# Attention slots with minima, biases added on GpSimd, and a division folded into the transposing matmul; decay and recurrent gates moved ahead of the index slots

## What is computed

```python
h = rms_norm(x, mix_norm)
x_r, g_r, q_b, c_kv, q_i, k_i, w_i, q_c, k_c, v_c, f_c, gate_a, gate_b, gate_c = split(h @ w_in)
o_a = rglru(x_r, g_r)        # conv of width 4, two gate matmuls, a scan over time
o_b = dsa(q_b, c_kv, ...)    # index scores relu(q_i.k_i) weighted by w_i, top 64 of them,
                             # softmax(ql.c * s + t5 bias, unselected at -1e30) @ c
o_c = fox(q_c, k_c, v_c)     # softmax(q.k * s + cum[t] - cum[key], causal) @ v
merged = sigmoid(gate_a)*(o_a @ w_b[0]) + sigmoid(gate_b)*(o_b @ w_b[1]) + sigmoid(gate_c)*(o_c @ w_b[2])
x = x + merged @ w_out
```

## Time and profile before

| | |
|---|---|
| median of 3 runs | 1520.07 us (1519.02 to 1524.56) |
| the profiled execution's own time | 1522.54 us |
| its span, first to last instruction | 1520.7 us |
| PE busy | 1448.3 us (95%) |
| DVE busy | 940.7 us (62%) |
| ACT busy | 785.6 us (52%) |
| POOL busy | 52.6 us (3%) |
| granted PE clock, mean over the span | 0.984 of full speed |

### The profile page before, as it was taken

How to read it: one execution, slowest core, us unless ns; L and a number is a source line. 1 busy time by engine, 2 the same in 40 slices (tenths; PEclk the granted TensorE clock), 3 DMA queues, 4 the chain that set the end, 5 groups by cost and what they waited for, 6 DMA issues and landing times.

```text
span 1520.7 us, 26191 instructions
## 1 busy us (share of the span) xinstructions
PE 1448.3 (95%) x9061; PEld 1290.7 (85%) x9061; DVE 940.7 (62%) x1501; ACT 785.6 (52%) x1396; POOL 52.6 (3%) x124
## 2 busy tenths in 40 slices
PE   6999999899999999999999999998999999999997
PEld 5888889788889897888878888888898898888886
DVE  5665655678665555666566666467875565565664
ACT  5555555644544455445465555456455445554553
POOL 1010000000000100000000000000000001000000
PEclk9999999899999999999999999999999999999999
DMA  7687655334424535566556666543353345356661
GB/s 224 192 201 218 201 150 157 117 116 141 138 91 162 192 112 163 173 189 193 167 175 186 193 185 199 158 141 112 112 166 111 111 170 164 112 172 192 190 193 70
DMA packets 286088, 243.60 MB, mean 160 GB/s; under 512 B 14281, under 2 KB 263545, under 8 KB 285985
## 3 DMA queue, kind: packets, MB, share of 16 engines
q1 hardware_dynamic: 283856, 236.77, 51.4%
q10 hardware_dynamic: 1600, 4.25, 0.8%
q0 software_dynamic: 528, 1.26, 0.6%
HBM read 241.18 MB, written 1.27 MB: 159 GB/s over the span
## 4 chain that ended last, share of the span: by engine, by line
issue 90%; PE 5%; POOLq 2%; POOL 1%; DMA 1%; DVE 0%; ACTq 0%; ACT 0%; DVEq 0%
PE work L1492 2%; PE work L1494 1%; PE acc L1454 1%; POOLq L685 1%; POOL diag L686 1%; POOLq L680 1%; DMA fb<-in_forget_bias 0%; POOLq L682 0%; DMA rows_dram<-brow_dram 0%; PE acc L1392 0%; DMA brow_dram<-brow 0%; POOL t L699 0%; POOL rstd L683 0%; DVE brow L1131 0%; ACTq L829 0%
## 5 line engine op out<-in xcount | busy, mean ns | idle before, releaser
L489 DVE TENSOR_TENSOR w_lo<-raw,w_hi 128x1024 fp32r<-128x1024 f32 x444 | 532.3, 1220 | 167.7 <-ACT w_hi L481 166.8
L1492 PE MATMUL work<-act,w_hi 128*128 128x512 f32 x1408 | 497.0, 397 | 2.6 <-DVE act L1031 2.6
L481 ACT ACTIVATE w_hi<-raw 128x1024 fp32r<-128x1024 f32 x444 | 453.4, 1053 | 39.0 <-PE acc L1454 26.4
L1494 PE MATMUL work<-act,w_lo 128*128 128x256 f32 x1408 | 395.0, 281 | 0.0
L1417 PE MATMUL work<-act,w_hi 128*128 128x256 f32 x1696 | 319.5, 287 | 9.0 <-DVE o_lo L1291 5.3
L1492 PEld LDWEIGHTS work<-act,w_hi 128*128 128x128 f32 x1408 | 264.2, 188 | 66.8 <-DVE act L1031 1.8
L1417 PEld LDWEIGHTS work<-act,w_hi 128*128 128x128 f32 x1696 | 270.3, 194 | 15.8 <-issue 9.6
L1494 PEld LDWEIGHTS work<-act,w_lo 128*128 128x128 f32 x1408 | 266.0, 189 | 1.5
L1417 PE MATMUL work<-act,w_lo 128*128 128x256 f32 x848 | 241.4, 285 | 0.0
L1417 PEld LDWEIGHTS work<-act,w_lo 128*128 128x128 f32 x848 | 164.3, 194 | 0.1
L741 ACT ACTIVATE gu_s<-work 128x256 f32<-128x256 f32 x176 | 58.0, 382 | 201.7 <-PE work L1494 201.7
(11 more groups left out here) (222 smaller groups left out, 1725.2 us busy)
## 6 DMA issues: line engine op xcount, KB each, us to landing
raw<-in_ffn_w_gu SPq DMA_DIRECT2D x176, 512.0 KB, 5.0
raw<-in_w_in SPq DMA_DIRECT2D x52, 1024.0 KB, 5.2
raw<-in_ffn_w_down SPq DMA_DIRECT2D x44, 1024.0 KB, 5.0
raw<-in_w_branch SPq DMA_DIRECT2D x12, 1024.0 KB, 5.0
raw<-in_w_mkv SPq DMA_DIRECT2D x8, 1024.0 KB, 5.0
raw<-in_w_out SPq DMA_DIRECT2D x8, 1024.0 KB, 5.0
raw<-in_w_mq SPq DMA_DIRECT2D x4, 1024.0 KB, 5.1
raw<-in_w_mo SPq DMA_DIRECT2D x4, 1024.0 KB, 4.8
```

What stands on the lines that cost most here:

```text
L481: eng.activation(halves(w_hi, slot, kind, part), halves(raw, slot, kind, part), ACT.Copy)\
L489: eng.tensor_tensor(halves(w_lo, slot, kind, part), halves(raw, slot, kind, part), halves(w_hi, slot, kind, part).bitcast(F32), ALU.subtra ...
L1492: pe.matmul(work[:, 2 * c + g, :], w_hi[:, slot, at_w:at_w + P], act[:, :, k, :], start=(k == 0), stop=False, skip_group_check=True)
L1494: mm = pe.matmul(work[:, 2 * c + g, 0:SEQ], w_lo[:, slot, at_w:at_w + P], act_hi[:, k, :], start=False, stop=(k == KT - 1), skip_group_che ...
```

## The change

- **Attention, DVE.** All logits are kept with the opposite sign, so that the row minimum is the bias of the exponential (`scale=-1.0`): `nm` comes straight from one `tensor_reduce` with `min`, and the negation goes. In fox the query's own `cum` is left out, since it is the same for all keys of a row and falls out of the softmax; `cum`, the job `cumT` and its copy go. POOL adds the causal mask to the second half of `fox_bias` once for each of the four pairs of heads, so slots with 256 keys need no mask on DVE; those with 128 keys add it in one instruction for both heads. In dsa POOL adds `t5` and `score` one slot ahead into `t5_score`.
- **Attention, division.** DVE only takes the reciprocal. POOL forms `over_sum`, a diagonal matrix of 1 / sum for each head (128 x 2 x 128), and PE multiplies the exponentials by it in ordinary matmuls in place of the transposes by the identity. PE's wait for `p_ready` becomes one for `over_sum_ready`.
- **Index stage.** `chan` moves behind `xr0`, and the convolution is done in two halves behind `xr0` and `xr1`. `rg` 0 and 1 and `fT` move ahead of `qi0`, `rg` 2 and 3 and `cT` ahead of `qi1`. The decay (sigmoid, running sum, store and broadcast load) and the gates' arithmetic on ACT and DVE move with them. The eight index slots now have a unit behind each second one. `dots` waits only for the half of `qi` that it reads, `qk` likewise. `rg_i` and `rg_a` lie over `merged` instead of `mem_x`.
- **Order of units.** `qc0, kc0, qc1, kc1` in place of `qc0, qc1, kc0, kc1`; `qb0, qb1` ahead of `ga0, ga1, ba0`. SP issues the loads in the new order; their number and sizes stay.

```diff
-FILL = dict(enumerate(("vc0", "vc1", "ga0", "ga1", "ba0", "qb0", "qb1", "ga2", "ga3", "ba1", "gc0", "gc1", "bc0",
+FILL = dict(enumerate(("vc0", "vc1", "qb0", "qb1", "ga0", "ga1", "ba0", "ga2", "ga3", "ba1", "gc0", "gc1", "bc0",
...
-IDX_FILL = {0: "qc0", 4: "qc1", 5: "kc0", 6: "kc1"}
+IDX_FILL = {1: "qc0", 3: "kc0", 5: "qc1", 7: "kc1"}
...
+            def causal_bias(pr):
+                h = HEAD_PAIRS[pr][0]
+                heads = fox_bias[:, h:h + 3:2, P:SEQ]
+                g.tensor_tensor(heads, heads, causal[:, P:SEQ].unsqueeze(1).to_broadcast([P, 2, P]), ALU.subtract)\
+                 .then_inc(causal_ready, 1)
+            def bias_and_score(l, s):
...
+                g.wait_ge(lg_ready, l * STREAM + s - 1)
+                g.tensor_tensor(t5_score[:, s % 2, :, 0:s_len], t5[:, h:h + 3:2, SEQ - s_len:SEQ],
+                                score[:, blk, 0:s_len].unsqueeze(1).to_broadcast([P, 2, s_len]), ALU.add)\
+                 .then_inc(t5_score_ready, 1)
...
+                for s in range(STREAM):
+                    if s == 0:
+                        g.wait_ge(bias_landed, l * 32 + 32)
+                        causal_bias(0)
+                    g.wait_ge(ri_ready, l * STREAM + s + 1)
+                    g.tensor_tensor(over_sum[:, s % 2, :, :], ident[:].unsqueeze(1).to_broadcast([P, 2, P]),
+                                    ri[:, s % 2, :].unsqueeze(2).to_broadcast([P, 2, P]), ALU.mult)\
+                     .then_inc(over_sum_ready, 1)
+                    if 0 < s < 4:
+                        causal_bias(s)
+                    if 8 <= s + 1 < STREAM:
+                        bias_and_score(l, s + 1)
...
-                            e = a.activation(lg[:, s % 2, j, 0:s_len], lg[:, s % 2, j, 0:s_len], ACT.Exp,
+                            e = a.activation(lg[:, s % 2, j, 0:s_len], lg[:, s % 2, j, 0:s_len], ACT.Exp, scale=-1.0,
...
-                        v.reduce_max(mx[:, s % 2, :], lgs, AX_X)
-                        v.drain()
-                        v.tensor_scalar(nm[:, s % 2, :], mx[:, s % 2, :], -1.0, None, ALU.mult).then_inc(lg_ready, 1)
+                        v.tensor_reduce(nm[:, s % 2, :], lgs, AX_X, ALU.min).then_inc(lg_ready, 1)
...
-                        v.reciprocal(ri[:, s % 2, :], sm[:, s % 2, :])
-                        v.drain()
-                        v.tensor_tensor(lgs, lgs, ri[:, s % 2, :].unsqueeze(2).to_broadcast([P, 2, s_len]), ALU.mult)\
-                         .then_inc(p_ready, 1)
+                        v.reciprocal(ri[:, s % 2, :], sm[:, s % 2, :]).then_inc(ri_ready, 1)
...
-                        pe.wait_ge(p_ready, l * STREAM + k + 1)
+                        pe.wait_ge(over_sum_ready, l * STREAM + k + 1)
...
-                                mm = pe.transpose(ps(("pt", k))[:, col:col + P], lg[:, k % 2, j, c * P:c * P + P], ident[:])
+                                mm = pe.matmul(ps(("pt", k))[:, col:col + P], lg[:, k % 2, j, c * P:c * P + P],
+                                               over_sum[:, k % 2, j, :], start=True, stop=True)
```

More of the change, by code:

```diff
@@ L156, in mix @@
         self.norm(1)
-        for name in ("xr0", "xr1", "gr0", "gr1"):
+        self.w_unit("xr0")
+        self.job("chan")
+        for name in ("xr1", "gr0", "gr1"):
             self.w_unit(name)
@@ L162, in mix @@
         self.job_of["misc"] = "nat"
-        self.job("chan")
-        for name in ("qi0", "qi1"):
-            self.w_unit(name)
+        self.job(("rg", 0))
+        self.job(("rg", 1))
+        self.job("fT")
+        self.w_unit("qi0")
+        self.job(("rg", 2))
+        self.job(("rg", 3))
+        self.job("cT")
+        self.w_unit("qi1")
         for i in range(IDX_SLOTS):
             self.job(("dots", i))
[L168 to L175, removed]
             if i in IDX_FILL:
@@ L275, in block_kernel @@
         merged = at("merged", [P, KT, SEQ])
+        rg_i = at("rg_i", [P, BT, SEQ], over="merged")
+        rg_a = at("rg_a", [P, BT, SEQ], over="merged", skip=4096)
         final_gain = at("final_gain", [P, D], over="merged")
@@ L289, in block_kernel @@
         qi = at("qi", [P, BT, SEQ])
+        over_sum = at("over_sum", [P, 2, 2, P], over="qi")
+        t5_score = at("t5_score", [P, 2, 2, SEQ], over="qc")
         vc = at("vc", [P, TT, BW])
@@ L336, in block_kernel @@
         wi = at("wi", [P, TT, HEADS])
-        cum = at("cum", [P, TT, HEADS])
         top8 = at("top8", [P, 8])
@@ L628, in _ @@
                   .then_inc(misc_landed, 16)
-                for name in ("qi0", "qi1") + tuple(IDX_FILL.values()):
+                for name in ("qi0", "qi1") + tuple(IDX_FILL[i] for i in sorted(IDX_FILL)):
                     w_in(l, name, COL[name[:2]] + 256 * int(name[2]))
@@ L1181, in _ @@
-                v.drain().then_inc(xc_ready, 1)
-                for j in range(2):
-                    splits(v, split_lo, l, f"qi{j}")
+                conv(0)
+                splits(v, split_lo, l, "xr1")
+                conv(1)
+                v.drain().then_inc(xc_ready, 1)
+                splits(v, split_lo, l, "gr0")
+                splits(v, split_lo, l, "gr1")
+                wait_done(v, l, "nat")
+                v.tensor_copy(nat[:], ps("nat")[:, 0:TT * NAT].rearrange("p (a n) -> p a n", a=TT))\
+                 .then_inc(bank_of("nat"), 1)
@@ new lines, in _ @@
+                for tt in range(TT):
+                    v.wait_ge(rstd_ready, l * 12 + 5 + tt)
+                    v.scalar_tensor_tensor(out=c_nat[:, tt, :], in0=nat[:, tt, HEADS:HEADS + LAT], scalar=rstd[:, tt:tt + 1],
+                                           in1=kvg[:], op0=ALU.mult,
+                                           op1=ALU.mult).then_inc(c_ready, 1)
+                v.wait_ge(fl_ready, l + 1)
+                v.scalar_tensor_tensor(out=f_l[:], in0=f_z[:], scalar=0.0, in1=f_l[:], op0=ALU.min, op1=ALU.subtract)
@@ L1184, in _ @@
+                v.tensor_tensor(xr[:, :, 0:SEQ], rg_a[:], rg_a[:], ALU.mult)
+                v.drain()
+                v.scalar_tensor_tensor(out=xr[:, :, 0:SEQ], in0=xr[:, :, 0:SEQ], scalar=1.0, in1=rg_r[:],
+                                       op0=ALU.add, op1=ALU.mult).then_inc(rg_v, 1)
+                splits(v, split_lo, l, "qi1")
                 for i in range(IDX_SLOTS):
@@ L1572, in _ @@
                     s_len = P * (blk + 1)
-                    wait_jobs(pe, l, ["ki", "qi0", "qi1"], ("dots", i))
+                    wait_jobs(pe, l, ["ki", f"qi{m // 2}"], ("dots", i))
                     for j in range(2):
```

279 lines of the change are left out of this document (131 added, 148 removed).

## The result

The changed kernel takes 1483.81 us (median of 4 runs, 1479.98 to 1487.17), the kernel before 1519.82 us on the same chip (4 runs, 1519.02 to 1524.56). The ratio is 0.9756 [0.9724, 0.9788]: 2.4% faster, 36 us.

What follows compares the result with a forecast made beforehand. PE, busy 95% of the span, was taken as the bound, losing time to waits and its lower clock. Terms -15.5 - 1 + 13.4 - 11.4 - 10 = -24.5 us, from the median 1520.07 to 1496 us; range 1486 to 1508.

Steps and rivals of the forecast that it cites:

- The waits: PE's waits in both layers: -15.5 us in the index stage and -11.4 us in the stream.
- the first `pt`: Start of the stream: PE still waits there for the softmax chain through DVE and POOL, 1.4 us in each layer.
- the `o_lo` waits: Stream, PE's four waits on DVE's reading of `uv`: 5.3 us before, to shrink to 1.1 us together.
- `qi1` and `qc0`: Index stage, two narrow places for ACT; rival: ACT falls behind there, +8 us, 1504 us, chance 0.08.
- The clock: PE in index stage and stream: 13 us lost at the lower clock, most returning once waits go, -10 us.
- the rival in which it doesn't: Rival: PE's granted clock falls as before, the 10 us are missing, 1506 us; chance 0.18.
- `cumT`: Index stage: four small matmuls per layer go from PE, -1 us.
- hidden in 30 of 32 slots: Stream: POOL's `over_sum`, 1.1 us (0.5 to 2.0), costs PE nothing except in the first step of each layer.
- the blocking rival: Stream: DVE and POOL block one another, delaying `over_sum` or DVE's reads; +6 to +9 us, 1502 to 1505, chance 0.12.
- the spare of 2.7 us: Stream, step 4: time between DVE's reciprocal and PE's `pt`, said to suffice for `over_sum` at 1.1 or 2.0 us.
- Transposes become matmuls: Stream, PE: 96 transposes become 192 matmul instructions, 23.8 - 10.4 = +13.4 us; ends +10.4 and +23.
- the low end of the range: Transposes at +10.4 us, all clock back, first waits half as long: 1488.6 us, put at 1486 for roundings.

Runs made afterwards that it cites:

- dve_divide: Changed kernel with the softmax division back on DVE, PE transposing by the identity, no `over_sum`, POOL's next bias beside the product: 1482.03 us, 0.9738 of the kernel before.
- dve_divide_2: As `dve_divide`, but POOL starts the next slot's bias only when DVE's product is done: 1478.65 us, 0.9711 of the kernel before.
- dots_apart: Changed kernel with index units behind slots 0, 2, 4, 6 and head pairs reordered so neighbouring `dots` read the same half of the partitions: 1495.14 us, 0.9817.
- early_softmax: As `dve_divide`, with DVE doing slot 0's logits and minimum ahead of the split for the last index unit: 1479.06 us, 0.9711 of the kernel before.
- divide_ordered: As `dve_divide_2`, with DVE's first softmax early and half of some fillers' splits moved behind what PE waits for: 1481.07 us, 0.9715.

## Why the prediction was right in direction and too small

**Right, and of the right size.** The waits: -27.6 us for a predicted -26.9. So good a match is partly luck. After the change 5.7 us are left where 3.9 were forecast, since the first `pt` waits 1.8 us in place of 1.4, the `o_lo` waits are 1.6 in sum in place of 1.1, and 0.5 for `vc` had no term; the other way went small gaps that the earlier trace rows doesn't list, 33.3 us before in place of the 30.8 counted. The index stage runs without a gap, so ACT did make `qi1` and `qc0` in time. The clock: `rg` and the units together take 10.1 us less, for a predicted 10. Not all of that need be the clock, but the clock's own record agrees: the stretches at the lower clock in the mixing parts sum to 37.5 us before and 10.2 after, and the matmuls in them to 32.8 and 10.4 us; at the prediction's 0.41 lost per us that is 13.4 us before and 4.3 after, 9 us back. `rg` had run mostly at the lower clock (9.3 of its 11.5 us), in between waits; what is left lies behind the wait at the first `pt`. That most of the clock comes back once the waits are gone, the forecast's least certain term, held, and the rival in which it doesn't is out. The four runs of the changed kernel still differ by their mean clock: 0.991, 0.994, 0.996 and 0.997 go with 1487.17, 1484.91, 1482.70 and 1479.98 us, 1.2 us per 0.001. `cumT`: -1.1 for -1.

**Right for the wrong part.** `over_sum` is hidden in 30 of 32 slots, as said. But its price isn't one number. One ahead of a half of `split_lo` (two SBUF inputs), and one with such a half beside it:

```profile
334.76 0.61 POOL L737 TENSOR_TENSOR over_sum<-ident,ri 128x256 f32<-128x256 f32 x1 [6.60 <-DVE ri L1325]
```

```profile
326.28 1.88 POOL L737 TENSOR_TENSOR over_sum<-ident,ri 128x256 f32<-128x256 f32 x1 [5.89 <-DVE ri L1325]
...
326.48 1.21 DVE L493 TENSOR_TENSOR w_lo<-raw,w_hi 128x1024 fp32r<-128x1024 f32 x1
```

Undisturbed it takes 0.61 us, not the 1.1 worked out from the earlier trace rows; behind DVE it takes up to 1.88, and the median of the 32 is 1.51. The estimate by the Trainium skill (GPSIMD Engine Reference, Elementwise), 0.6 us, was the better one for the undisturbed product; the trace agrees with it in 12 of the 32 slots. The lock is there in both directions: POOL's 0.61 grows to as much as 1.88 us beside the split's 1.21, and DVE's product goes from 0.69 to 1.83 us beside POOL's 1.29. The Trainium skill (SBUF — State Buffer, two separate sides) says that such operations of the two engines exclude one another for a whole instruction, and that the one that starts first goes first; the traces agree on the first point. On the second the recorded starts need care: a split that starts 0.15 us ahead of POOL's record makes POOL's product 1.51 to 1.55 us long, one that starts 0.20 us behind it 1.88, and only one that starts 0.41 us or more behind leaves POOL its 0.61, with the split then at 1.21 to 1.28.

So the mechanism of the blocking rival is real and its price wasn't: the spare of 2.7 us from the earlier trace rows takes 1.88, and in the changed kernel POOL bears the delay nearly alone, for none of the 444 halves of `split_lo` takes more than 1.285 us (1.227 before). Nor is the blocking part of the wait at the first `pt`, where `over_sum` takes 0.61 us in both layers (start 296.16, `pt` at 296.90 in the first). Only with the product back on DVE did the blocking cost time, 3.2 us of waits (`dve_divide` against `dve_divide_2`).

**The terms that failed.** The mechanism held; what failed is the sum, in a term that it didn't have and in one that was too large. The excess is 35.4 - 24.5 = 10.9 us.

- **`dots`, -4.5 us, no term at all.** The prediction said that a unit stands behind each pair of `dots` and asked only what that does to ACT. It took the 64 matmuls as the same work at the same price. The trace of before had the warning, which I didn't read: twelve instructions of three slots in a row take 263.88 - 262.79 = 1.09 us, where the four of a slot alone take 0.64 (256.85 - 256.22).

```profile
256.22 0.71 PE L1575 MATMUL work<-ki,qi 64*128 64x128 f32 x4 [0.69 <-ACT qi L734]
256.85 0.38 PE L1417 MATMUL work<-act,w_hi 128*128 128x256 f32 x1
...
262.79 1.16 PE L1575 MATMUL work<-ki,qi 64*128 64x128 f32 x12
263.88 0.44 PE L1582 MATMUL work<-ident,c_nat 128*128 128x128 f32 x2
```

This is the largest part of the miss, and `dots_apart` shows how it hangs on the neighbours: with the two slots of a pair on the same half the 64 instructions take 12.2 us.
- **Transposes become matmuls, +13.4, measured +11.0.** The 192 instructions cost 23.4 us, for 23.8 predicted; the mistake is in what they replace. I took 0.108 us for each of the 96 transposes, from one slot with 256 keys in the middle of a burst; over all slots they took 12.4 us, 0.129 each. The row was the cheapest of its kind: the sixteen slots with four transposes took 0.43 to 0.53 us, 0.121 for each transpose on average, and those with two 0.146 for each, among them two right behind PE's wait (310.19 to 310.56 in the trace of before, 0.185 each).
- **Small jobs around them, -2.2 us**, in `cT`, `fT`, `pv`, `uv` and `ql`, no term. All of them ran at the full clock before too, so the clock isn't the cause. `cT` and `fT` make 0.9 of it: the two matmuls of `cT` counted 0.44 us ahead of a wait before and 255.26 - 255.12 = 0.14 us in a row with the next unit after. The other 1.3 us stay open; no run separates them.
- **Waits -0.7 and outside the mixing part -1.0 us**, neither larger than what single executions differ by.

Together 4.5 + 2.4 + 2.2 + 0.7 + 1.0 = 10.8 of the 10.9 us; the clock and `cumT` make the rest. All terms that failed lay on one side, and the low end of the range (transposes at 10.4, all clock, half the first waits) had no room for work that becomes cheaper without being touched.

**What the parts are worth.** The order of the index stage gives 1.7% of the 2.4% by itself. The folded division, which the prediction counted as the price of the change, isn't bought back by what DVE saves: with the product back on DVE and POOL behind it, the kernel takes 1478.65 us against 1485.56. With POOL beside it (`dve_divide`, 0.9738) the gain isn't clear of the intervals. `dve_divide_2` and `early_softmax` (0.9711 each) are the fastest versions that compute the whole, with `divide_ordered` (0.9715) within their intervals.

## What to carry to other kernels

When work is regrouped, price the untouched small matmuls anew: who their neighbour is can halve them, and a group of several in a row in the old trace can show it. A wait for a bank is a sign of who is late, not of what to remove: taking `cumT` out alone moved 9.3 us to the next thing that DVE owed. And where PE is 95% busy, an instruction added to PE to relieve an engine that is 62% busy must remove waits of its own size; here 11 us were paid, and 11 - 6.9 = 4 us came back.

## What the hardware showed that I had not expected

- fp32 matmuls that contract 64 partitions run at the same time when neighbours use opposite halves of the partitions: eight instructions in 1.07 us against 1.92 on one half (256 columns), 0.65 against 1.08 (128 columns).
- A DVE product of 128x512 took 1.83 us beside a POOL operation of 1.29 us and 0.69 alone; POOL's 128x256 product took 0.61 to 1.88 us by when DVE's split of 1.21 us started, with the border between 0.20 and 0.41 us behind POOL's recorded start.
- The granted clock differs from run to run of one kernel (0.991 to 0.997 here), with 7 us between the ends; no difference below that can be read from two single profiles.
